# Values tile by tile, x asked for later, table loads without a wait between them

## The reference

```python
for l in range(DEPTH):
    sh1, sc1, g1, sh2, sc2, g2 = adaln(c, w_ada[l], b_ada[l])
    hs = modulate(rms_norm(xs, norm_g[l, 0]), sh1, sc1)
    if l % 2 == 0:
        q, k, v = jnp.split(hs @ w_qkv[i], 3, axis=-1)
        s_loc = einsum(q, k_window) * HEAD_DIM ** -0.5 + bias      # bias: rpb table, -inf outside
        p = softmax(concat([s_loc, s_ctx])); ys = (p @ v) @ w_o[i]
    ...
    xs = xs + g1 * ys
    xs = xs + g2 * sq_relu_mlp(modulate(rms_norm(xs, norm_g[l, 1]), sh2, sc2), w_up[l], w_down[l])
```

## Time and profile before

| | |
|---|---|
| median of 3 runs | 2685.6 us |
| the runs | 2671.91, 2685.6, 2939.64 us |
| profiled execution | 2670.14 us |
| its span, core 0 (slowest) | 2668.6 us |
| spans of all cores | 2657.3 to 2668.6 us |
| TensorE busy | 2445.8 us, 92% |
| VectorE busy | 1107.2 us, 41% |
| ScalarE busy | 1051.0 us, 39% |
| GpSimd busy | 336.8 us, 13% |
| packets in the engines, GpSimd's queue | 41.4% |
| packets in the engines, SP's queue | 4.7% |

### The profile page before, as it was taken

The page is one execution under the profiler, slowest core; times in us unless marked ns, Lnnn a source line. Parts: engine busy times, 40 slices in busy tenths (PEclk is TensorE's granted clock), DMA queues, the critical chain, the costliest instruction groups (busy, mean ns, idle before and its releaser), DMA issues.

```text
span 2668.6 us, 41955 instructions; the slowest of 8 cores (2657.3 to 2668.6 us)
## 1 busy us (share of the span) xinstructions
PE 2445.8 (92%) x14955; PEld 1077.7 (40%) x15184; DVE 1107.2 (41%) x1552; ACT 1051.0 (39%) x1563; POOL 336.8 (13%) x395
## 2 busy tenths in 40 slices
PE   2888889999999988999999888899999998899998
PEld 1322224444444443444443222344444454344443
DVE  1344444422325565323244554443232555632333
ACT  3455555301224466202254555551031445730224
POOL 1122220000001141000002322000000112200000
PEclk8999989999999989999999999899999998999999
DMA  9765533455543212555438444156664331233432
GB/s 208 149 87 69 71 57 62 78 99 100 99 76 68 54 29 48 102 101 98 79 73 155 56 56 56 20 76 101 99 101 72 61 60 31 32 48 50 55 54 95
DMA packets 133434, 205.99 MB, mean 77 GB/s; under 512 B 73136, under 2 KB 79280, under 8 KB 132464
## 3 DMA queue, kind: packets, MB, share of 16 engines
q0 software_dynamic: 109872, 161.70, 41.4%
q1 hardware_dynamic: 23360, 41.60, 4.7%
HBM read 322.89 MB, written 31.46 MB: 133 GB/s over the span
## 4 chain that ended last, share of the span: by engine, by line
PE 77%; DMA 6%; ACT 6%; issue 5%; DVE 5%; POOL 1%; DVEq 0%; ACTq 0%; POOLq 0%; SPq 0%
PE pp L654 23%; PE ps L654 19%; PE pp L677 7%; PE ps L884 4%; PE pp L1276 3%; DMA scr<-rpbp 3%; PE pp L1003 2%; PE ps L677 2%; PE pp L1404 2%; PE ps L1028 2%; PE ps L1276 2%; PE pp L1239 2%; PE ps L582 2%; DMA ring<-wall 2%; DVE scr L976 1%
## 5 line engine op out<-in xcount | busy, mean ns | idle before, releaser
L723 DVE TENSOR_TENSOR big<-big 128x512 bf16<-128x512 f32 x384 | 265.5, 692 | 415.8 <-ACT big L721 415.8
L654 PE MATMUL ps<-hTs,ring 128*128 128x512 bf16 x1488 | 339.0, 383 | 13.5 <-ACT hTs L632 8.5
L654 PE MATMUL pp<-hTs,ring 128*128 128x512 bf16 x1520 | 342.7, 380 | 1.9
L419 POOL DMA_DIRECT2D ring<-wall x140 | 99.1, 708 | 1712.7 <-PE pp L654 492.9
L654 PE MATMUL pp<-big,ring 128*128 128x512 bf16 x1362 | 304.9, 379 | 2.8 <-ACT big L721 1.2
L721 ACT ACTIVATE big<-ps 128x512 f32<-128x512 f32 x190 | 113.2, 596 | 472.5 <-PE ps L654 468.2
L575 ACT ACTIVATE scr<-xTs 128x512 bf16<-128x512 f32 x216 | 133.3, 626 | 318.8 <-DVE xTs L693 277.0
L693 DVE SCALAR_TENSOR_TENSOR xTs<-pp,mod,xTs 128x512 f32<-128x512 f32 x156 | 116.8, 750 | 330.2 <-PE pp L654 239.4
L976 DVE TENSOR_TENSOR scr<-pp,scr 128x768 f32<-128x768 f32 (+2 forms) x192 | 174.5, 910 | 143.1 <-PE pp L1009 69.3
L721 ACT ACTIVATE big<-pp 128x512 f32<-128x512 f32 x194 | 115.4, 596 | 296.7 <-PE pp L654 293.8
L654 PEld LDWEIGHTS ps<-hTs,ring 128*128 128x128 bf16 x1520 | 148.6, 98 | 192.3 <-issue 18.7
(11 more groups left out here) (120 smaller groups left out, 2689.8 us busy)
## 6 DMA issues: line engine op xcount, KB each, us to landing
ring<-wall POOLq DMA_DIRECT2D x140, 1024.0 KB, 11.2
vo<-big SPq DMA_DIRECT2D x48, 256.0 KB, 5.6
kTo<-big SPq DMA_DIRECT2D x48, 256.0 KB, 2.1
scr<-rpbp POOLq DMA_DIRECT2D x64, 128.0 KB, 3.6
xTs<-xT SPq DMA_DIRECT2D x3, 2048.0 KB, 19.8
yT<-scr SPq DMA_DIRECT2D x24, 256.0 KB, 2.2
scr<-big SPq DMA_DIRECT2D x64, 54.0 KB, 6.8
scr<-big POOLq DMA_DIRECT2D x64, 54.0 KB, 6.8
```

The source lines that it names most:

```text
L654: ins = e.matmul(ps[pi][:, :], lhsT=w[:, kc, fc * fw:(fc + 1) * fw], rhs=src[:, kc, t * 512:(t + 1) * 512], start=(kc == 0), stop=(kc == n ...
L723: P.op("dve", lambda e: e.tensor_tensor(out=hid[:, hc, t * 512:(t + 1) * 512], in0=ta[:, :], in1=ta[:, :], op=ALU.mult), reads=[ta_r], wri ...
```

## The change

Four edits. (1) x tile 1 waits for piece 3, as tile 2 does, and no longer for piece 2. (2) The value products run tile by tile: for each tile the four blocks with value piece 0, then the four with value piece 1. Both pieces are held until tile 2; their `done_piece` come behind blocks 8 to 11 of each. (3) In layer 0 the squares of the next tile are no longer called whole: five before the first of four groups, three before the third, during (tile 0, piece 1) for tile 1 and during (tile 1, piece 0) for tile 2; the products with ones follow some groups behind. (4) Each of the four table loads has a semaphore and a `Res` of its own, for every head pair; the first loads stand before the last four groups, the first mask behind the last.

```diff
-            extra=[[], [(ring_sem[2], 16)], [(ring_sem[0], 32)]][t])
+            extra=[[], [(ring_sem[0], 32)], [(ring_sem[0], 32)]][t])
...
-            Tsem.extend(P.new_sem(f"T{l}_{n}") for n in range(2))
+            for ap, r in Tb:
+                parts = [r] + [Res(f"Tp{k}", init=scr.inherit) for k in range(3)]
+                scr.live.extend(parts[1:])
+                Tp.append(parts)
+            Tsem.extend([P.new_sem(f"T{l}_{n}_{k}") for k in range(4)] for n in range(2))
...
-                        Tsem[hp % 2], writes=[Tt_r])
+                        Tsem[hp % 2][2 * par + rl], writes=[Tp[hp % 2][2 * par + rl]])
...
-                reads=[Tt_r, vecs_r], writes=[Tt_r])
+                reads=tp + [vecs_r], writes=tp)
...
-        for j in range(2):
-            s = use_piece("v", l, j)
-            for b in range(12):
-                t = b // 4
-                if l == 0 and j == 0 and b in (0, 4):
-                    ensure_h(b // 4)
-                    norm_whole(b // 4 + 1)
-                if b % 4 == 0:
-                    ensure_h(t)
+        vslots = [use_piece("v", l, j) for j in range(2)]
+        for t, j in [(t, j) for t in range(NT) for j in range(2)]:
+            s = vslots[j]
+            if j == 0:
+                ensure_h(t)
+            if (t, j) == (2, 1):
+                scr_begin()
+                load_T(0)
+            for b in range(4 * t, 4 * t + 4):
+                if l == 0 and (t, j) in ((0, 1), (1, 0)) and b % 2 == 0:
+                    for c in range(5) if b % 4 == 0 else range(5, 8):
+                        norm_chunk(ctx0, c, t + 1, 2 if c < 5 else 1)
                 pi = next_ps()
...
-            done_piece()
-            if j == 0:
-                scr_begin()
-                load_T(0)
-                mask_T(0)
+            if t == 2:
+                done_piece()
+        mask_T(0)
...
-                    reads=[ps_r[2 * pp], ps_r[2 * pp + 1], Tt_r], writes=[z_r])
+                    reads=[ps_r[2 * pp], ps_r[2 * pp + 1]] + tp, writes=[z_r])
```

More of the change, by code:

```diff
@@ L775, in attn_layer @@
         rcp = wr[:, 0:1024].bitcast(F32)
-        zb, pT, Tb = [], [], []
+        zb, pT, Tb, Tp = [], [], [], []
         st_sem = [P.new_sem(f"st{l}_{n}") for n in range(4 + 2)]
@@ L805, in load_T @@
         def load_T(hp):
-            Tt, Tt_r = Tb[hp % 2]
+            Tt = Tb[hp % 2][0]
             for par in range(2):
@@ L813, in load_T @@
                         out=Tt[64 * rl:64 * rl + 64, par, :].rearrange("p (o q) -> p o q", o=16), in_=src),
-                        Tsem[hp % 2], writes=[Tt_r])
+                        Tsem[hp % 2][2 * par + rl], writes=[Tp[hp % 2][2 * par + rl]])
         def mask_T(hp):
-            Tt, Tt_r = Tb[hp % 2]
+            Tt, tp = Tb[hp % 2][0], Tp[hp % 2]
             v = Tt[:, :, :].rearrange("p h (o q) -> p (h o) q", o=16)
```

## The result

| | before | changed |
|---|---|---|
| median, 19 runs each | 2674.48 us | 2689.92 us |
| profiled execution | 2670.14 us | 2684.61 us |
| spans of its cores | 2657.3 to 2668.6 us | 2674.6 to 2683.1 us |
| mean of the eight spans | 2664.9 us | 2678.6 us |

In some executions of either kernel the cores of one die run slower, and the ratio leaves these out. The changed kernel is slower by 0.76%: the ratio of its times to those of before, run side by side, is 1.0076, with a 95% interval of 1.0055 to 1.0097, about 15 to 26 us. That is well inside two per cent, so it counts as no change by that bound, but the interval excludes 1. The forecast was 2678 us with 2660 to 2696 around it; the median lies 12 us above it, inside the range and outside my own case's range of 2672 to 2686. Against the profiled execution of before the forecast was +7.7 us; the profiled pair shows +14.5.

A forecast was written before the change was run, and what follows sets the result against it. Mostly TensorE-bound; before attention, weight pieces, x tile 1, serial table loads and the mask bound it. Mask lateness of 7.3 us in layer 0 plus 0.4 in layer 2 gave +7.7 on 2670.1, so 2677.8 us, range 2660 to 2696.

The forecast's parts named there:

- my own case: Whole program: the main forecast, 2672 to 2686 us from the bounds of stores and tables; chance 0.42.
- The later request: Start of layer 0: x tile 1 lands at 59.2 us instead of 53.0, value piece 0 at about 48.5 instead of 54.9.
- The store wait: Layer 0 values: fifth evacuation waits until 71.8 us for the first store, behind x tile 2; tile 1 ready at 86.8.
- The first rival: Layer 0 values: stores are no obstacle, values end at 111.7 us (-3.7), total 2668 us; chance 0.22.
- 121.5 us instead of 115.4, +6.1: Layer 0: end of the value products on TensorE, 6.1 us later than before.
- +7.3 against 132.3: Layer 0: first mask ends at 139.6 us, 7.3 us later, carried whole into the program's sum.
- The table loads: Before the first mask: independent loads take 25 us from weight piece issue to mask end instead of 36.9; bounds 22 and 36.9.
- the rival that they are not: Table loads no quicker together: mask +19 us in layer 0, +12 in layer 2, total 2702 us; chance 0.03.
- The gain of 12 us is used up by the later place: Table loads: independence gains 12 us, but they start 8 groups later in the order.
- Layer 2: Layer 2 values: the 0.95 us stop goes, the mask ends at 1442.9 us against 1442.5, +0.4.
- The rival with the K stores: Head pairs: bursts of four table loads delay K stores, 14 pairs of 4 us, total 2726 us; chance 0.02.
- The clock: Layer 0 values: stops before tiles 1 and 2 keep the clock at 1.2 GHz, +14 us, total 2692; chance 0.07.

The follow-up runs named there:

- e_eight: Changed kernel with eight staging buffers for the values instead of four; ratio to before 1.0059.
- e_actq: Changed kernel with the first four value stores of layer 0 issued by ScalarE instead of SP; no ratio, profiled execution 2694.41 us.
- after_again: The changed kernel run once more without an edit, as reference for the other runs; ratio to before 1.0079.
- e_tserial: Changed kernel with the four table loads waiting for one another again, at their new place; ratio to before 1.0123.
- e_b_indep: Kernel before with independent table loads alone, everything else in its old place; ratio to before 0.9997.
- e_tearly: Changed kernel with the first table loads of a layer before tile 2's first group instead of behind the fourth; ratio to before 1.0085.
- c_all: Changed kernel with eight value staging buffers and the first table loads before tile 2's first group; ratio to before 1.005.
- c_all_k: Changed kernel with eight value buffers, table loads before tile 2's first group, and three own buffers for pair 0's K evacuations; ratio to before 1.0004.

## Why the prediction was right or wrong

**The later request: right.** On core 0 the values started at 47.8 us (48.5 forecast) and the groups of value piece 1 at 59.0 (60). x tile 1 landed at 57.1 us (59.2), x tile 2 at 68.9 us (71 to 72), by the list of DMA issues from 39.5 us:

```profile
xTs<-xT SPq DMA_DIRECT2D x1, 2048.0 KB, 29.8
```

**The store wait: right in place and size on core 0, its mechanism half right.** Fifth evacuation at 71.01 us (71.8), tile 1's groups at 85.74 (86.8), tile 2's at 105.99 (107.2), end of the values at 121.36 (121.5). The last figure agrees partly by luck: tile 2 was ready 1.2 us earlier, and its eight groups took 15.4 us instead of 14.3 (see the clock below). The forecast also left out the stop of 4.77 us of before, so that more than "the whole stop of 4.43 us" stood there to be saved. The first rival, that the stores are no obstacle, is excluded by that and by e_eight. I put the wait down to x tile 2 standing in front in SP's queue. The four stores do land right behind it, at 70.9, 71.5, 72.2 and 72.8 us; but e_actq shows that without x in front only the first is sooner, and that the others are late because the engines are full.

**The size for the whole program: wrong, and this is the step that failed.** "**121.5 us instead of 115.4, +6.1**" and "The mask ends at 139.6, **+7.3 against 132.3**" were worked out on core 0 of one execution, against that core's own past, and the sum took +7.3 for the program. In the mean over the cores the values' term is +9.4 instead of +6.1, and the mask's end +15.5 instead of +7.3. The missing 8.2 us have three parts. The mask of before ended at 129.4 us in the mean and not at 132.3, since core 0 had the latest of the eight (the others 125.3 to 130.7): 2.9 us. The values ended at 123.9 us and not at 121.5: 2.4 us. The mask ended 21.0 us behind the values and not 18.1: 2.9 us, which is the term of the table loads. The 2.4 us come from the transfers: on the other seven cores x tile 2 landed at 70.3 to 71.5 us instead of 68.9, the first store 2.0 to 2.8 us behind it, and the fifth evacuation started at 73.4 us in their mean instead of 71.0. So the working fitted core 0 and was 5.3 us short for the others, beside the wrong reference point of 2.9 us.

That core 0's span then grew by 6.0 us (2668.6 to 2674.6), near the forecast, is luck, and core 0 is no special core. Its mask came 8.5 us later, and 3.6 us of that came back in the eight pairs, where the forecast had the delay carry over one for one. And in the executions that the ratios rest on and whose spans are on record (41 of before, 18 of the changed kernel) its span has a median of 2662.7 us before and 2681.8 now, +19, and the mean of the eight spans one of 2662.8 and 2682.2. The profiled execution of before had core 0 about 6 us above its usual span, that of the changed kernel 7 us below. All eight cores of the one profile of before were there to be read, and would have given the 2.9 us.

**The table loads: right in direction, 1 to 5 us too quick.** "I take 25", from the issue of the weight piece in front to the end of the mask: 25.7 us on core 0 (115.17 to 140.85), 30.1 on core 6 (119.42 to 149.53), 27.2 in the mean (28.8 in after_again), within the bounds of 22 and 36.9. I had the weight piece in front "less disturbed by other transfers"; on core 6 the second piece, asked for 7 us behind it, and nine stores lay beside them. That loads together are quicker is shown by e_tserial, which excludes the rival that they are not. "The gain of 12 us is used up by the later place" held in its second half. The gain of one layer was put too high: with serial loads at the new place the first mask ends 6.6 to 8.8 us later, and the 12 us of e_tserial are what both layers cost together. At the old place the gain could not be had either (e_b_indep).

**The mask's move behind the reload: right,** nothing. **Layer 2: right on core 0.** The stop of 0.95 us is gone. The mask ends at 1447.8 us, 5.3 later than in the earlier trace rows, and 4.9 of that was there already at layer 0's output projection (410.29 to 415.17), which leaves +0.4, as forecast. In the mean over the cores the same difference is -0.3 us.

**The rival with the K stores.** It was given 0.02, on the ground that K evacuations and bursts of loads are far apart in each pair. For the later pairs that was right: the stretch of eight pairs kept its length (275.1 and 273.7 us). For pair 0 it was wrong. There the K stores fall among two weight pieces, four table loads and the value stores, and land in 6.9 to 12.3 us instead of 2.7. In the changed kernel this hides behind the mask; e_tearly and c_all show it standing right behind, and c_all_k shows its price, 9 us in layer 0 and 8 at layer 2's attention start, 3 of which come back behind it (1710.4 - 1448.3 = 262.1 us to the projection, and 265.2). I had priced 14 pairs and not the first.

**The clock.** No such loss as the rival's 14 us, but a small part of it. The granted clock of core 0 between 60 and 90 us was 0.83 before and 0.72 now, from the windows view (length; busy time of PE, PEld, DVE, ACT and POOL with counts; granted clock; DMA share; GB/s):

```profile
60.00:90.00 30.00, 14.42 (x51) 5.36 (x49) 8.59 (x13) 14.22 (x24) 2.15 (x3) 0.72 0.75 170
```

After each of the stops the first group costs more: the next row starts 3.17 us behind 85.74 us and 3.28 us behind 105.99 us, where a group costs 1.74 us at the full clock. The forecast counted that at tile 1 (two groups in 5.06 us) and not at tile 2, about 1 us. On core 6 two groups at 61.90 us took 5.30 us where core 0 took 3.61; that costs nothing, because TensorE stands 7.21 us for a norm soon behind them.

**What stays open.** The runs show about 20 us, the first profiled pair 14.5 and 13.7 in the mean of its spans. Most of the difference is which executions were profiled: the mean span of before was 2 us above its median, that of the changed kernel 4 us below. The second profile of the changed kernel has a mean span of 2683.7, 18.8 above before, with its mask wait 1.7 and its layer 2 some 3 us longer. Why executions differ so was not looked into. Which transfers beside the second weight piece hold the K stores was not settled, nor why the stretch from the projection of layer 0 to layer 2 differs by a microsecond or two from kernel to kernel.

## What to carry to other kernels

Work a forecast out on every core, or on their mean: the slowest core of one profile may be the slowest in that execution only, and its waits are then longer than the usual ones. When a wait is taken away, look which instruction would be late next and read the landing time of what it waits for in the new surroundings, not in the old ones; here the K store stood behind the mask within half a microsecond. Small stores out of few staging buffers beside large loads hold the engine that evacuates, so free the buffers first, and only then move the work.

## What the runs showed of the hardware that I had not expected

A store of 256 KB that lands in 2.7 us when the engines have room took 17.5 to 21.2 us beside two queues of large transfers (the first four of the changed kernel, core 6). A queue of its own shortened only the first, to 12.9 us; the other three took 18.1 to 19.3. The window of 60 to 62 us shows why: the three queues got 39, 41 and 41 packets, and 0.16, 0.34 and 0.08 MB, since a packet of the stores is 2 KB and those of weights and x are larger (4.1 KB and 8.3 KB by these numbers). In these runs turns are given by packet, so the transfer in small packets gets the least bytes; the earlier trace rows has the same equal counts, 238 and 237, for two queues. Four table loads issued within 3.3 us took 20 to 25 us from the first issue to the last landing beside weights and stores in layer 0 of the changed kernel, of which 2.2 us each are their own work.
